# A two-block transformer kernel: the differential heads' norm from one tile of roots, and two products ahead of the experts' jump

## The reference

```python
y_attn = diff_attention(q, k, v, lam, lam_init, diff_subln_g[l])   # 8 heads of width 128
#   inside, for each head and token:
#   o = o * lax.rsqrt(jnp.mean(jnp.square(o), axis=-1, keepdims=True) + RMS_EPS)
#   o = o * subln_g * (1.0 - lam_init)
y_conv = short_gated_conv(cb, cc, cu, conv_w[l])
y_mem = memory_attention(qm, mem, w_mem_kv[l])
g = jax.nn.sigmoid(gates.reshape(B, S, N_BRANCH, D))
merged = g0 * (y_attn @ w_br_attn[l]) + g1 * (y_conv @ w_br_conv[l]) + g2 * (y_mem @ w_br_mem[l])
x = layer_norm(DEEPNORM_ALPHA * x + merged @ w_out[l], ln1_g[l], ln1_b[l])
f = grouped_moe(x, ...)                                             # 16 experts, 2 for each token
x = layer_norm(DEEPNORM_ALPHA * x + f, ln2_g[l], ln2_b[l])
```

## Time and profile before

| | us |
|---|---|
| median of three runs | 2249.02 (2247.35 to 2249.37) |
| profiled execution | 2250.36 |
| its span, first to last instruction | 2248.4 |
| TensorE (PE) busy | 2200.8 (98%) |
| VectorE (DVE) busy | 1144.9 (51%) |
| ScalarE (ACT) busy | 436.5 (19%) |
| mean granted TensorE clock, as a share | 0.997 |

### The profile page before, as it was taken

The page is one execution under the profiler, slowest core; times in us unless marked ns, Lnnn a source line. Parts: engine busy times, 40 slices in busy tenths (PEclk is TensorE's granted clock), DMA queues, the critical chain, the costliest instruction groups (busy, mean ns, idle before and its releaser), DMA issues.

```text
span 2248.4 us, 24692 instructions
## 1 busy us (share of the span) xinstructions
PE 2200.8 (98%) x9803; PEld 1392.6 (62%) x9803; DVE 1144.9 (51%) x1926; ACT 436.5 (19%) x988; POOL 3.1 (0%) x20
## 2 busy tenths in 40 slices
PE   9999999999999999999999999999999999999998
PEld 7755444544458765446444486788888888554453
DVE  3765775211137267763111237775456423587666
ACT  2001401211121014212111146420000002252110
POOL 0000000000000000000000000000000000000000
PEclk9999999999999999999999999999999999999999
DMA  8345934799983439436999912002222224403340
GB/s 351 146 183 219 384 139 172 296 398 427 428 366 121 179 150 409 190 150 231 394 427 427 420 46 113 1 1 98 90 75 82 78 103 166 189 10 150 140 178 19
DMA packets 45262, 457.93 MB, mean 204 GB/s; under 512 B 5416, under 2 KB 15706, under 8 KB 17498
## 3 DMA queue, kind: packets, MB, share of 16 engines
q1 hardware_dynamic: 35520, 449.85, 49.6%
q10 hardware_dynamic: 9626, 6.46, 0.9%
HBM read 455.15 MB, written 1.15 MB: 203 GB/s over the span
## 4 chain that ended last, share of the span: by engine, by line
PE 83%; DVE 7%; DMA 7%; DVEq 2%; issue 1%; ACT 1%; SPq 0%; POOLq 0%; POOL 0%; ACTq 0%
PE banks L603 80%; DMA ring<-in_w_exp_up 7%; PE banks L1714 1%; PE banks L759 1%; DVE ring L3030 1%; DVE tiny L3241 1%; DVE tiny L2579 1%; DVE arena L2593 0%; DVE arena L3256 0%; DVE ring L2324 0%; DVE arena L2298 0%; DVE banks L2576 0%; DVEq L2299 0%; PE banks L1190 0%; DVEq L2592 0%
## 5 line engine op out<-in xcount | busy, mean ns | idle before, releaser
L603 PE MATMUL banks<-ring,arena 128*64 128x512 f32 (+2 forms) x3302 | 960.7, 546 | 14.1 <-DMA ring<-in_w_exp_up 4.4
L603 PEld LDWEIGHTS banks<-ring,arena 128*128 128x128 f32 (+1 forms) x3302 | 449.5, 166 | 484.5 <-issue 449.9
L603 PE MATMUL banks<-arena 128*128 128x128 f32 (+7 forms) x1584 | 243.9, 344 | 3.7 <-issue 1.7
L603 PE MATMUL banks<-X,ring 128*128 128x256 f32 x1024 | 223.6, 380 | 0.5 <-DVE arena L2532 0.5
L603 PEld LDWEIGHTS banks<-X,ring 128*128 128x128 f32 x1024 | 195.0, 191 | 29.1 <-issue 2.3
L603 PEld LDWEIGHTS banks<-arena 128*128 128x128 f32 (+2 forms) x1584 | 155.3, 173 | 66.5 <-issue 34.4
L603 PE MATMUL banks<-arena,ring 128*128 128x256 f32 (+1 forms) x736 | 178.8, 399 | 0.1
L603 PEld LDWEIGHTS banks<-arena,ring 128*128 128x128 f32 x736 | 138.9, 190 | 36.7 <-issue 15.3
L2423 DVE TENSOR_TENSOR arena<-arena,banks 128x512 f32<-128x512 f32 x16 | 11.0, 687 | 278.7 <-ACT arena L1873 278.7
L603 PE MATMUL banks<-ring 128*128 128x256 f32 x616 | 137.0, 379 | 0.0
L603 PEld LDWEIGHTS banks<-ring 128*128 128x128 f32 x616 | 117.0, 190 | 15.9
(11 more groups left out here) (367 smaller groups left out, 1883.7 us busy)
## 6 DMA issues: line engine op xcount, KB each, us to landing
ring<-in_w_in SPq DMA_DIRECT2D x38, 2048.0 KB, 11.9
ring<-in_w_exp_up SPq DMA_DIRECT2D x32, 2048.0 KB, 16.4
ring<-in_w_exp_down SPq DMA_DIRECT2D x32, 2048.0 KB, 11.9
ring<-in_w_exp_gate SPq DMA_DIRECT2D x30, 2048.0 KB, 13.5
ring<-in_w_ada SPq DMA_DIRECT2D x24, 2048.0 KB, 11.0
ring<-in_w_ffn SPq DMA_DIRECT2D x22, 2048.0 KB, 7.7
ring<-in_w_out SPq DMA_DIRECT2D x8, 2048.0 KB, 13.1
ring<-in_w_down SPq DMA_DIRECT2D x8, 1408.0 KB, 5.9
```

The costliest lines, as they stand in the source:

```text
L603: ins = nc.tensor.matmul(out, weights, moving, start=start, stop=stop)
```

## The change

With `mean_d[:, 0:32]` as weights each head tile gives 32 equal rows of sums, and the four tiles go to partitions 0, 32, 64 and 96 of bank 4. One variance, one root and one reciprocal over that 128x512 tile (`diff_roots`) serve all heads. `roots_spread` brings the four rows back to 128 partitions: for each a matmul of depth one, with a row of ones as weights, into a bank of its own. It stands in `token_blocks` between the two blocks of tokens, and VectorE multiplies `oT` out of these banks. The second part puts the two products that need nothing of the experts inside both paths of the branch, behind `last_scatter`; counters that both paths must leave alike are saved and restored with them (not shown).

```diff
+        diff_squares, diff_roots = [view(2048 + 512 * i, 512) for i in range(HEADS // 2)], view(2048, 512)
+        SPREAD_BANKS = (7, 0, 1, 6)
...
-            def token_blocks(src, width):
+            def token_blocks(src, width, between):
                 w = slot(next_tile(), CC, D)
                 for tc in range(TC):
+                    if tc:
+                        between()
                     for half in range(2):
...
                 def head_sums():
-                    for hp in range(HEADS // 2):
-                        norm_sums([view(2048 + 512 * hp, 512)], 512, mean_d, 4 + hp % 2, s_square)
+                    free(4)
+                    for i, squares in enumerate(diff_squares):
+                        pe.wait_ge(s_square, C.next("square"))
+                        ins = mm(bank[4][32 * i:32 * i + 32, :], mean_d[:, 0:32], squares, start=True, stop=True,
+                                 more=(i < 3))
+                    full(ins, 4, "dve")
+
+                def roots_spread():
+                    pe.wait_ge(s_diff_inv, l + 1)
+                    for i, b in enumerate(SPREAD_BANKS):
+                        free(b)
+                        full(mm(bank[b][:], ones[32 * i:32 * i + 1, :], diff_roots[32 * i:32 * i + 1, :],
+                                start=True, stop=True), b, "dve")
                 unit(X, x_sums2, summed=ROWS_SUMMED[l] + 4 - l, between=head_sums)
-                token_blocks(ymT, 256 if l else 512)
+                token_blocks(ymT, 256 if l else 512, roots_spread)
...
+                def next_products():
+                    if l == DEPTH - 1:
+                        context_chunk(4)
+                        context_chunk(6)
+                        return None
+                    w = slot(next_tile(), DC, 512)
+                    for c in range(2):
+                        feature_product(w, c, memT, T, "act")
+                    return w
...
                 with pe.If(more < 1):
                     last_scatter()
+                    next_products()
                     pe.sem_inc(o_used, PAIRS * N_OVER)
                 with pe.Else():
...
+                    w = next_products()
...
-                if l == DEPTH - 1:
-                    context_chunk(4)
-                    context_chunk(6)
-                    normed_rows_turned()
-                else:
-                    w = slot(next_tile(), DC, 512)
-                    for c in range(MEM_HEADS):
-                        if c == 2:
-                            normed_rows_turned()
+                normed_rows_turned()
+                if l < DEPTH - 1:
+                    for c in range(2, MEM_HEADS):
                         feature_product(w, c, memT, T, "act")
                     used()
...
-                for v, _ in heads:
-                    root(v)
+                root(diff_roots)
...
                 def head_variances():
-                    for i, (r, _) in enumerate(heads):
-                        variance(4 + i % 2, r, RMS_EPS, 512, D / P)
-
-                def head_norm(i):
-                    r, o_ = heads[i]
-                    inverse(r)
-                    stt(o_, o_, subg[:, ds(l, 1)], r, ALU.mult, ALU.mult)
+                    variance(4, diff_roots, RMS_EPS, 512, D / P)
+
+                def head_inverses():
+                    inverse(diff_roots)
+                    drain().then_inc(s_diff_inv, 1)
                 def heads_normed():
-                    head_norm(3)
                     drain().then_inc(s_attn_out, 1)
...
                 unit(UNIT_SLOTS[l][4], rows(gates), more=(head_variances,),
-                     filler=(lambda: head_norm(0), lambda: head_norm(1)))
+                     filler=(head_inverses,))
                 dve.wait_ge(s_branch_gate, C.next("branch_gate", 2 * TC))
                 for i in range(2 * TC):
+                    if i == TC:
+                        for n, b in enumerate(SPREAD_BANKS):
+                            filled()
+                            o_ = oT[:, 2 * n:2 * n + 2, :].rearrange("p a t -> p (a t)")
+                            done(stt(o_, o_, subg[:, ds(l, 1)], bank[b][:], ALU.mult, ALU.mult))
                     g = rows(gates)(i // 2, i % 2)
                     done(tt(g, take()[:], g, ALU.mult))
                 drain()
                 tt(merged, merged, gates, ALU.add)
-                head_norm(2)
                 unit(UNIT_SLOTS[l][5], rows(gates), filler=(heads_normed,))
```

More of the change, by code:

```diff
@@ L217, in build @@
         s_head_inv = sem("head_inverse_roots_ready")
+        s_diff_inv = sem("differential_head_inverse_roots_ready")
         ring = sb("ring", [P, RING, TILE])
@@ L1303, in _ @@
                 more, last_scatter = expert_pairs()
-                begun = (dict(C.k), dict(last), unsent[0])
+                def next_products():
[7 more added lines that the diff above has]
+                    return w
+                begun = (dict(C.k), dict(last), unsent[0], at[0], dict(turn))
                 with pe.If(more < 1):
                     last_scatter()
+                    next_products()
                     pe.sem_inc(o_used, PAIRS * N_OVER)
@@ L1310, in _ @@
                 with pe.Else():
-                    C.k, unsent[0] = dict(begun[0]), begun[2]
+                    C.k, unsent[0], at[0] = dict(begun[0]), begun[2], begun[3]
+                    turn.update(begun[4])
                     last.clear()
@@ L1321, in _ @@
                             pe.drain().then_inc(o_used, 1)
-                last.clear()
-                last.update(held)
+                    w = next_products()
+                for b, read in held.items():
+                    last.setdefault(b, read)
                 settle(pe)
@@ L1958, in _ @@
                 act.wait_ge(s_heads, C.next("heads"))
-                heads = [(view(2048 + 512 * i, 512), oT[:, 2 * i:2 * i + 2, :].rearrange("p a t -> p (a t)"))
-                         for i in range(HEADS // 2)]
-                squares(heads)
+                squares([(dst, oT[:, 2 * i:2 * i + 2, :].rearrange("p a t -> p (a t)"))
+                         for i, dst in enumerate(diff_squares)])
                 first_product()
-                for v, _ in heads:
-                    root(v)
+                root(diff_roots)
                 branch_gates()
```

## The result

The change made the kernel slower. The median of 20 runs is 2251.65 us, against 2249.01 us of the kernel before in as many runs beside them: a ratio of 1.0014, 95% interval [1.0008, 1.002]. The forecast was 2243.2 us, with a range of 2240.0 to 2247.3 us. The profiled execution took 2250.1 us.

A forecast was written before the change was run, and what follows sets the result against it. The kernel was taken as a string of TensorE matmuls (83% of the chain). Layer 0's 2.63 us, layer 1's 3.00 and the jumps' 0.2 make 5.8 us, so the median goes from 2249.02 to 2243.2 us, range 2240.0 to 2247.3.

The forecast's parts named there:

- The head sums: Differential heads' norm on TensorE: four 128-row matmuls become four of 32 rows, saving 2.62 us (layer 0) and 2.63 us (layer 1).
- The spread: Four added depth-one matmuls between the token product's halves cost 1.07 us per layer, bounds 0.86 and 3.44 us.
- VectorE's queue: Bank 2 is read 1.8 us before TensorE asks, closing the gap: 1.08 us gained in layer 0, 1.44 us in layer 1.
- The experts' jump: Two products moved ahead of the jump gain 0.1 us per layer; bounds nothing and 0.3 us for both layers.
- The clock: Granted-clock falls at the routers may shift: one step of 1.6 us per layer either way, 3.2 us altogether.
- first: Rival at the spread: depth-one products do not overlap, taking 3.44 us, not 1.07; 2247.9 us, chance 0.11.
- second: Rival ahead of the token product: TensorE still waits for bank 2, 2.5 us not gained; 2245.7 us, chance 0.10.
- third: Rival at the experts' loads: the gain is waited for again, only the jumps' 0.2 us left; 2248.8 us, chance 0.06.
- fourth: Rival at the new products: the clock falls, 3.4 us at each of four places, +7.8 us; 2256.8 us, chance 0.03.

The follow-up runs named there:

- e1: The kernel before with only the head norm's part of the diff, the experts' jump left as it was; 2243.12 us, ratio 0.9973.
- e2: The kernel before with only the two products put ahead of the jump and copied into the other path; 2256.26 us, ratio 1.0034.
- e3: The kernel before with 64 semaphore increments, never run, added at the end of the path not taken; 2258.83 us, ratio 1.0044.
- e9: The kernel before with a jumped-over fill right ahead of the jump, meant to put it at place 200 of a 256 block; 2265.04 us, ratio 1.0073.
- e10: The kernel before with a jumped-over fill right ahead of the jump, offset 0 of a 256 block, as control; 2263.58 us, ratio 1.0064.
- e11: The changed kernel, last scatter products once ahead of the branch, plus a jumped-over fill to place 165 before TensorE's first wait; 2248.20 us, ratio 0.9995.
- e13: The changed kernel, last scatter products once ahead of the branch, plus a jumped-over fill to place 200 before TensorE's first wait; 2244.77 us, ratio 0.9983.
- e4: The changed kernel with 95 semaphore increments run at TensorE's start; 2261.59 us, ratio 1.0057 to the kernel before.
- e5: The changed kernel with 175 semaphore increments run at TensorE's start; 2271.80 us, ratio 1.0103 to the kernel before.
- e7: The changed kernel with the last scatter products hoisted ahead of the branch, once for both paths; 2252.55 us, ratio 1.0015 to the kernel before.
- e14: The changed kernel, last scatter products once ahead of the branch, plus a jumped-over fill to place 222 before TensorE's first wait; 2246.95 us, ratio 0.9992.
- e6: The changed kernel, last scatter products once ahead of the branch, plus 145 semaphore increments run at TensorE's start; 2263.03 us, ratio 1.0064.
- e12: The changed kernel, last scatter products once ahead of the branch, plus a jumped-over fill ahead of the two moved products; 2250.95 us, ratio 1.0009.
- e8: The changed kernel with a jumped-over fill, offset 0 of a 256 block, right ahead of the jump; 2254.93 us, ratio 1.0032.

## Why the prediction was wrong

**The head sums** were right: 2.63 us saved in layer 0 (3.62 less 0.99), by 2.62 forecast.

**The spread** was right: 1.07 us to the next start in both layers. The nearest row, 32 deep, was a good measure for depth one, down to the 0.21 us over perfect overlap. But the start of the next product is not the whole price. The products next to the sums and the spread take 0.1 us longer too: in layer 0 13.84 us for the 32 records behind the sums where 13.74 stood, and 13.93 for the token product's 32, less the spread, where 13.81 stood. The sum left this out. Together with the 0.14 and 0.21 us over perfect overlap that is 0.2 to 0.3 us for each, and what they go to is not shown.

**VectorE's queue** was right: bank 2 was read well before it was asked for, and neither layer has a gap ahead of the token product, where 1.08 and 1.44 us stood.

These terms make 5.6 us. e1 measures them alone at 6.0, give or take 2.5. The stretch up to the oT unit shows 5.2: the missing 0.4 are the four times 0.1 us next to the sums and the spreads.

**The experts' jump** was the step that failed. I wrote "No work is added or removed on the path taken. I take 0.1 us per layer", and bounded it by 0 and 0.3 us. The first sentence was true and beside the point. Both bounds came from a row in which the jump was free. Its 0.11 us are not even the jump's: with the jump gone from that place, the changed kernel still takes 0.96 us from the scatter product to the next (645.44 to 646.40), where 0.97 stood. And I carried the row over to a jump whose target the change had moved. The diff put a second copy of the products into the path not taken, between the jump and its target. The measured term is +5.6 us of stalls and +1.7 us of clock in the profiled execution (+7.2 us in e2), where -0.2 stood. The bound from the other side would have been a whole fetch, which no row of the trace before shows (a full miss is 5.4 to 6.0 us by e3, e9 and e10); but queue 8's 81 packets of code, 1.33 MB, were on the page. That was a rival that I did not write: a jump that misses in both layers with 3 us hidden, as now measured, and the forecast's 2243.2 becomes 2243.2 + 0.2 + 5.6 + 1.7 = 2250.7 us.

**The clock**: my allowance of one step either way per layer was right in kind. The granted clock stands at 1.00 or at 0.50 in the trace's records; before it is at 0.50 for 3.41 us in layer 0 and 6.83 us in layer 1, so the 1.7 and 3.4 us lost of the earlier trace rows, and at each router of the changed kernel it is for one of these two lengths. The routers' two falls changed places (mean 0.88 and 0.76 before, 0.76 and 0.88 after) for no net change. The third fall came from a place that I had not looked at, behind the stall.

**The rivals**: depth one overlaps (first, out). The gap is closed (second, out). The experts don't swallow the gain (third): e1 keeps it whole. The clock does not fall at the new products (fourth): the stretch of 268 to 300 us of the changed kernel has a granted clock of 1.00.

```profile
268.00:300.00 32.00, 32.00 (x86) 13.34 (x86) 21.47 (x20) 6.24 (x8) 0.00 (x0) 1.00 0.46 189
```

The side was right in that rival, slower, and its mechanism was not the one that acted.

## What to carry to other kernels

Code that never runs can have a price if a taken jump passes over it (64 instructions never run cost 9.8 us in e3), so count the instructions between a jump and its target, and the block in which they lie, not only the work on the path taken; an idle stretch that ends with "issue" 1.3 to 1.8 us after a packet of queue 8 has landed was that price in all 22 holes here, and for one at the jump the jump's own record shows how long it took (6.12 us for a hole of 2.59). Run the parts of a change apart before believing its sum: one part here was worth 6.0 us and the other cost 7.2. And after an edit of code ahead of such a jump expect a few us either way that have nothing to do with the edit: here 35 places took a stall of 2.79 us away (e11, e13).

## What the runs showed of the hardware

- A jump without a miss costs nothing that the starts show: 0.96 us from the last scatter product to the next in the changed kernel, with no jump between them, and 0.97 in the kernel before, with one, whose own record takes 0.31 us. A whole miss costs 5.4 to 6.0 us of idle TensorE (e3 in layer 1, e9, e10), by the jump's record 5.6 to 6.4 us.
- In all 22 holes of 1.6 us or more at or behind the jumps, over all traces, one packet of queue 8 ends 1.3 to 1.8 us before TensorE goes on. In the five whole misses it starts 2.7 to 3.3 us after the hole opens, in the changed kernel within 0.4 us of the opening. So some 3 us of a miss are hidden there: the jump's record starts 3.84 and 3.87 us before the matmuls issued ahead of it end.
- A jump without a hole is not always a short one: its record takes 3.15 and 2.15 us in e13, all of it under matmuls, and 0.40 and 0.29 us in e1.
- Queue 8 brings 16,384 bytes for every 256.0 to 257.2 records of TensorE (sixteen traces, 1420 to 2200 us).
- The same instructions shifted by a few dozen places stall at the jump in one layer, the other, both or none: 2.49 us in layer 0 alone (e4) and 2.33 us in layer 1 alone (e5), where the changed kernel has 2.59 and 2.99; with the hoisted scatter 2.71 and 2.73 us in both (e7), 2.79 us in layer 0 alone (e11), none (e13, e14).
- A hole can come behind the target as well, 1.6 to 2.8 us (e3, e5, e6, e12, e14). That the target then lies near the end of the last block at hand is a count, not a measurement.
- A jump that starts 0.4 to 0.5 us behind the start of the fill's branch waits wherever it was put: its record takes 6.32 and 6.16 us in e9, 5.59 and 6.19 in e10, where the kernel before has 0.31 and 0.39. With 4.0 us between them (e12) it takes 2.42 and 2.00 us. The reason given is the reading that fits e8, e10 and e12; no run isolates it.
- A semaphore increment on TensorE's queue took 0.153 us at the kernel's start (e4, e5; e6 agrees).
- The granted clock can fall with such a stall: 0.81 over 655 to 664 us with a stall of 2.59 us in the changed kernel, but 1.00 from 1280 to 1305 us with one of 2.99 us. Of the 22 holes, 17 have a fall to a granted clock of 0.50 in them or shortly behind, and 5 have none. A stall alone doesn't decide it, and what does was not tried.
